# A decoder step on one Trainium2 core: first combine from the samples' tile, block vectors asked for in another order

## The reference

```python
for layer in range(DEPTH):
    np_ = rmsnorm(xp, norm_mix[layer]); ns_ = rmsnorm(xs, norm_mix[layer])
    mp, ms = mixer(np_), mixer(ns_)          # layer 0 attention, layer 1 s5_mix
    xp = xp + mp; xs = xs + ms
    xp = xp + hier_moe(rmsnorm(xp, norm_ffn[layer]), *moe_w)
    xs = xs + hier_moe(rmsnorm(xs, norm_ffn[layer]), *moe_w)
y_prompt = rmsnorm(xp, norm_final)
```

## Time and profile before

| | us |
|---|---|
| median of 3 runs | 935.3 |
| lowest, highest | 932.11, 938.24 |
| profiled execution | 935.06 |
| its span | 933.3 |

### The profile page before, as it was taken

How to read it: one execution, slowest core, us unless ns; L and a number is a source line. 1 busy time by engine, 2 the same in 40 slices (tenths; PEclk the granted TensorE clock), 3 DMA queues, 4 the chain that set the end, 5 groups by cost and what they waited for, 6 DMA issues and landing times.

```text
span 933.3 us, 12709 instructions
## 1 busy us (share of the span) xinstructions
PE 759.3 (81%) x4843; PEld 471.9 (51%) x4843; DVE 405.6 (43%) x1001; ACT 260.0 (28%) x554; POOL 151.7 (16%) x233
## 2 busy tenths in 40 slices
PE   3899977988999889997800599899999889999730
PEld 2344445857545775554500477544345487555420
DVE  3378695866678441111155567301112262111118
ACT  6020035644122102322231356310014412232203
POOL 1010003000868012332000201000000001333110
PEclk9999996999999799999965799899999979999875
DMA  9462135000632898999789377780131296999936
GB/s 343 138 210 89 51 137 192 2 1 7 217 136 114 331 408 330 408 411 403 272 280 316 44 193 185 198 325 0 45 135 46 75 402 246 405 409 406 375 138 226
DMA packets 75382, 201.81 MB, mean 216 GB/s; under 512 B 14873, under 2 KB 29593, under 8 KB 74265
## 3 DMA queue, kind: packets, MB, share of 16 engines
q1 hardware_dynamic: 58360, 161.77, 48.1%
q0 software_dynamic: 9696, 19.75, 6.0%
q10 hardware_dynamic: 7264, 19.46, 5.7%
HBM read 171.64 MB, written 39.39 MB: 226 GB/s over the span
## 4 chain that ended last, share of the span: by engine, by line
PE 61%; DMA 14%; DVE 10%; ACT 7%; SPq 4%; issue 2%; PEldq 0%; POOL 0%; DVEq 0%; PEld 0%; POOLq 0%; ACTq 0%
PE PSUM L2025 14%; PE PSUM L1832 9%; PE PSUM L1617 8%; PE PSUM L1776 7%; PE PSUM L1853 4%; DMA RING<-in_moe_w_up 3%; DMA RING<-in_attn_w_qkv 3%; PE PSUM L1820 3%; PE PSUM L1574 2%; DMA PH<-in_moe_w_up 2%; DVE X L1495 2%; DMA RING<-XNT 2%; PE PSUM L1975 2%; PE PSUM L1971 2%; SPq L467 2%
## 5 line engine op out<-in xcount | busy, mean ns | idle before, releaser
L1617 PE MATMUL PSUM<-RING,XNT 128*128 128x512 f32 (+2 forms) x256 | 94.5, 567 | 4.1 <-DMA RING<-in_attn_w_qkv 3.4
L1832 PE MATMUL PSUM<-PH 128*64 128x256 f32 x448 | 87.4, 404 | 9.0 <-DMA PH<-in_moe_w_up 5.1
L2025 PE MATMUL PSUM<-PH,XNT 128*128 128x512 f32 (+1 forms) x220 | 88.1, 593 | 0.3 <-PE PSUM L2025 0.3
L657 POOL DMA_INDIRECT PH<-xn_scratch,PH x32 | 32.6, 1020 | 340.7 <-DVEq L1440 247.5
L1832 PE MATMUL PSUM<-RING,PH 128*64 128x256 f32 x384 | 71.2, 398 | 9.7 <-DMA PH<-in_moe_w_up 5.0
L1471 DVE TENSOR_TENSOR PH<-PH,PSUM 128x128 f32<-128x128 f32 x32 | 9.3, 289 | 137.1 <-ACT PH L962 137.1
L1617 PEld LDWEIGHTS PSUM<-RING,XNT 128*128 128x128 f32 (+1 forms) x256 | 40.4, 177 | 53.7 <-issue 47.7
L1832 PEld LDWEIGHTS PSUM<-PH 128*64 128x64 f32 x448 | 52.4, 146 | 28.3 <-issue 12.5
L1776 PE MATMUL PSUM<-RING,PH 128*128 128x512 f32 (+1 forms) x160 | 62.6, 593 | 0.0
L2025 PEld LDWEIGHTS PSUM<-PH,XNT 128*128 128x128 f32 (+1 forms) x220 | 36.4, 180 | 47.9 <-issue 47.8
L1556 DVE TENSOR_TENSOR PH<-PSUM,PH 128x512 f32<-128x512 f32 (+1 forms) x10 | 6.9, 690 | 116.4 <-ACT PH L1066 116.4
(11 more groups left out here) (378 smaller groups left out, 1359.3 us busy)
## 6 DMA issues: line engine op xcount, KB each, us to landing
PH<-in_moe_w_gate SPq DMA_DIRECT2D x28, 512.0 KB
PH<-in_moe_w_up SPq DMA_DIRECT2D x28, 512.0 KB
RING<-in_moe_w_gate SPq DMA_DIRECT2D x24, 512.0 KB
RING<-in_moe_w_up SPq DMA_DIRECT2D x24, 512.0 KB
RING<-in_moe_w_down SPq DMA_DIRECT2D x24, 512.0 KB
PH<-in_moe_w_down SPq DMA_DIRECT2D x24, 512.0 KB
RING<-in_attn_w_qkv SPq DMA_DIRECT2D x4, 1536.0 KB
XNT<-in_moe_w_gate SPq DMA_DIRECT2D x12, 512.0 KB
```

The source lines that it names most:

```text
L657: pool.indirect_dma_start(out=XG[:, i % 2, :], out_offset=None, in_=xn_d[layer], in_offset=bass.IndirectOffsetOnAxis(ap=IDX[:, i:i + 1], a ...
L1617: last = te.matmul(PSUM[lo:hi, b0 + col // 512, col % 512:col % 512 + n], XT[:, c, t * P:t * P + r], RING[:, c // 2, (c % 2) * QKV + col:( ...
L1832: last = te.matmul(PSUM[m * 64:(m + 1) * 64, 2 + i % 2, 0:2 * FF], XGT[:, i % 2, c, m * 64:(m + 1) * 64], gu[:, :, c, :], start=(c == 0), ...
L2025: last = te.matmul(PSUM[p0:p0 + r, 2 * (i % 2) + w, :], XT[:, c, t * P:t * P + r], slot(SLOT[q])[:, (2 * (c % 3) + w) * 512:(2 * (c % 3) + ...
```

## The change

Five edits. `TILES` gives the norm of layer 0's combine (n = 2) the tile order 4, 0, 1, 2, 3: the row loads, DVE's additions, both halves of the norm and the copies to AL go in that order, and `place` numbers the semaphores' values accordingly; all other norms keep theirs. SP loads two blocks' vectors behind the row loads and the other two behind the copies to AL. ACT asks for the fifth block's vectors in iteration 3 behind the copies of U, and no longer in iteration 2 behind the copies of the taps; the sixth to eighth stay. PE waits for the tenth `x_updated` (the last addition) and runs `keep_busy(16, 7)` ahead of the end of phase 4. PE runs `keep_busy(10, 7)` in iteration 0 between the transposes of W and the wait for the gather.

```diff
+        TILES = {2: (4, 0, 1, 2, 3)}
+        def tiles(n):
+            return TILES.get(n, range(NT))
+        def place(n, t):
+            return NT * n + list(tiles(n)).index(t)
         block = ctx.enter_context(nc.Block())
...
                 sp.wait_ge(S("all_stored"), layer + 1)
-                for t in range(NT):
+                for t in tiles(2 + 2 * layer):
                     sp.dma_start(YG[t][0:ROWS[t], :, :],
...
             sp.dma_start(in_d[:, 2 * GP * CH:], PWRQ.rearrange("p r k g -> p (r k g)")).then_inc(S("bb_out"), 16)
+            def block_in(k):
+                ring_load(Q_SSM + k, [(slot(SLOT[Q_SSM + k])[:, 0:BLK_F], blk_d[k])])
             experts(0)
...
             rows_back(0)
-            for k in range(4):
-                ring_load(Q_SSM + k, [(slot(SLOT[Q_SSM + k])[:, 0:BLK_F], blk_d[k])])
-            for t in range(NT):
-                sp.wait_ge(S("xn_done"), 2 * NT + t + 1)
+            for k in (0, 1):
+                block_in(k)
+            for t in tiles(2):
+                sp.wait_ge(S("xn_done"), place(2, t) + 1)
                 rows = AL[t:PCH:4, :, :] if t < 4 else AL[PCH:NCH, :, :]
                 sp.dma_start(rows, XN[0:ROWS[t], t, :]).then_inc(S("al_in"), 16)
+            for k in (2, 3):
+                block_in(k)
...
             else:
-                act.wait_ge(S("x_updated"), NT * (n - 1) + t + 1)
+                act.wait_ge(S("x_updated"), place(n, t) - NT + 1)
             r = ROWS[t]
...
                                  accum_out=SS[0:r, n, t:t + 1]).then_inc(S("squares"), 1)
-            act.wait_ge(S("squares"), NT * n + t + 1)
+            act.wait_ge(S("squares"), place(n, t) + 1)
             nc.scalar.activation(RSTD[0:r, n, t:t + 1], SS[0:r, n, t:t + 1], ACT.Sqrt, bias=EPSC[0:r, :],
...
         def norm_dve(dve, ch, n, t):
-            dve.wait_ge(S("roots"), NT * n + t + 1)
+            dve.wait_ge(S("roots"), place(n, t) + 1)
             r = ROWS[t]
             ch(nc.vector.reciprocal(RSTD[0:r, n, t:t + 1], RSTD[0:r, n, t:t + 1]))
-            if t == 0:
+            if t == tiles(n)[0]:
                 dve.wait_ge(S("gamma_in"), 16 * (n + 1))
...
                                          ).then_inc(S("hs_in"), 1)
-                for t in range(NT):
+                for t in tiles(2 + 2 * layer):
                     norm_act(act, 2 + 2 * layer, t)
...
             moe(0, 4)
+            def block_in(k):
+                q = Q_SSM + k
+                act.wait_ge(S("ring_free"), freed(q))
+                act.dma_start(slot(SLOT[q])[:, 0:BLK_F], blk_d[k]).then_inc(S(f"ring_full{SLOT[q]}"), 16)
...
                     nc.scalar.activation(uk[:, :, 0:NSEQ], ut[:, :, PCH:NCH], ACT.Copy).then_inc(S("u_ready"), 1)
+                    if k == 3:
+                        block_in(4)
                 if 2 <= k < NB + 2:
...
                     ins.then_inc(S("kp_ready"), 1)
-                    if 4 <= k + 2 < NB:
-                        q = Q_SSM + k + 2
-                        act.wait_ge(S("ring_free"), freed(q))
-                        act.dma_start(slot(SLOT[q])[:, 0:BLK_F], blk_d[k + 2]).then_inc(S(f"ring_full{SLOT[q]}"), 16)
+                    if 5 <= k + 2 < NB:
+                        block_in(k + 2)
                 if k >= 3:
...
                                            ).then_inc(S("ov_dve"), 1)
-                for t in range(NT):
+                norm = 2 + 2 * layer
+                for j, t in enumerate(tiles(norm)):
                     r = ROWS[t]
...
                                                 in1=X[0:r, t, :], op0=ALU.mult, op1=ALU.add).then_inc(S("yg_used"), 1)
-                        dve.wait_ge(S("yg_used"), (layer * NT + t) * 2 + k + 1)
+                        dve.wait_ge(S("yg_used"), (layer * NT + j) * 2 + k + 1)
                     dve.sem_inc(S("x_updated"), 1)
-                    if t:
-                        norm_dve(dve, ch, 2 + 2 * layer, t - 1)
-                norm_dve(dve, ch, 2 + 2 * layer, NT - 1)
+                    if j:
+                        norm_dve(dve, ch, norm, tiles(norm)[j - 1])
+                norm_dve(dve, ch, norm, tiles(norm)[-1])
                 end_phase(dve, ph)
...
                     last.then_inc(S("st_transposed"), 1)
+                    pe.wait_ge(S("x_updated"), 2 * NT)
+                    keep_busy(16, 7)
                 end_phase(pe, ph)
...
                 last.then_inc(S("w_transposed"), 1)
+                if k == 0:
+                    keep_busy(10, 7)
                 pe.wait_ge(S("u_gathered"), k + 1)
...
                     pe.wait_ge(S("u_ready"), k)
```

## The result

The changed kernel takes 929.62 us (median of 13 runs, 925.76 to 938.66), the kernel before 934.65 us (13 runs, 931.68 to 945.91). The ratio is 0.9942, with a 95% interval of 0.9916 to 0.9969: by the ratio 5.4 us less, between 2.9 and 7.9. It is faster, but by less than the 1% that the prediction set for "faster", and by half of the forecast 11.2 us. The time lies in the range of 920 to 931 us. The profiled execution took 925.76 us (span 923.8), the shortest of the 13, so its stages stand at the favourable end.

What follows compares the result with a forecast made beforehand. The prediction took a DMA queue, carrying XN's tiles into AL behind four blocks' loads, to bound the seam. Terms -7.2 - 3.0 - 0.7 - 1.0 + 0.7 = -11.2 took 935.06 to 923.9 us; range 920 to 931.

Steps and rivals of the forecast that it cites:

- the seam: Between layer 0's experts and the state-space loop: 19.44 us waiting on XN's transfer into AL, expected to become 6 to 8.
- the fifth block later: In the loop: its later-requested load lands 0.9 us after its transposes' present start, costing +0.7 us, bounds 0 and +2.
- the forecast's own part: Total time if the forecast holds, without the rivals: 920 to 926.5 us around 923.9, chance 0.62.
- rival one: At the copies to AL: full tiles serialise behind the samples' tile, taking 15.3 us; total 929.5 us, chance 0.20.
- Two blocks moved behind the tiles: In SP's queue: 3.01 MB no longer stand ahead of the tiles, -7.2 us; what the moved blocks meet costs nothing.
- the start-up: At the first row loads: 1.2 us of slow starting, which could hide the samples' slow load; 0.7 counted, 0.5 left.
- The samples' tile first: At the copies to AL: it holds half the engines while others move full tiles; 10.75 us instead of 13.75, -3.0.
- its row load first: At the combine's row loads: the samples' slow load falls into the start-up, -0.7 us, between 0 and -1.2.
- The fillers: On PE before the loop: they keep the clock up, so the first block runs at 2.4 GHz, -1.0 us.
- rival two: In the loop: the fifth block's load meets shift pieces and sixth block, landing 4 us late; 927.2 us, chance 0.08.

Runs made afterwards that it cites:

- split_only: The kernel before with only its third and fourth blocks' loads moved behind the tiles' copies; 927.84 us, ratio 0.9925.
- natural_order: The changed kernel with layer 0's combine tiles in order 0 to 4 again, the samples' tile last; 934.32 us, ratio 0.9976.
- one_ahead: The changed kernel with only one block's vectors loaded ahead of the tiles' copies and three behind; 929.98 us, ratio 0.9942.
- fifth_old_again: A repeat, with a second profile, of the changed kernel with the fifth block's load back at its old place in iteration 2; 926.64 us, ratio 0.9903.
- fifth_old_place: The changed kernel with the fifth block's load back at its old place, behind the KP copies of iteration 2; 924.16 us, ratio 0.9854.

## Why the prediction was half right

The mechanism of the seam was right, the sum there a little large, and one step behind it, *the fifth block later*, was sized wrongly by far. The time lies within 920 to 931 us only because that range was stretched over the rivals; the forecast's own part ended at 926.5. That 929.62 us is the time of rival one (929.5) is chance: the tiles did not serialise, and GpSimd's copy came 36.6 us behind the first row load, 509.3 in the times of the earlier trace rows, between the forecast's 507.5 and the rival's 511 to 512. Point by point:

- **Two blocks moved behind the tiles, -7.2.** The blocks end 7.7 us earlier (7.2 and 0.5 of the start-up). Alone, in the natural order of the tiles, it brought 5.7 us (split_only): there it is not so that what the moved blocks meet costs nothing. Queued behind the samples' tile as the last one, they lengthen its tail, 15.4 us for the tiles instead of 13.75 (natural_order).
- **The samples' tile first, -3.0, and its row load first, -0.7.** Together 2.6 to 3.4 us at the seam (natural_order against the profiles of the changed kernel), near the 3.7. But not for the reason given: the tiles take 12.6 us, not 10.75, because the samples' tile ahead of the others holds all engines at 120 GB/s for 5 us. The half share that I argued from the earlier trace rows was that of a transfer with nothing behind it. Rival one's 15.3 us is further off on the other side, and its two instructions of 16 engines each do not fit the half share of the samples' tile in the earlier trace rows. The Trainium skill, "SBUF — State Buffer", section "Can I just issue two DMAs to hit both halves?", has two transfers to different partitions serialise nearly wholly. The 12.6 us lie between that and full overlap. The 1.7 us that the blocks add to a tail in the natural order make up the difference.
- **The fillers, -1.0: nothing.** The barrier fell near 505 and the last filler ended at 508.4, both as forecast when counted from the first row load (3.2 us later in this execution). But the rows came 5.2 us behind it instead of 3.2, because the seam was 1.9 us longer than forecast. The clock stayed at 1.00 through 4.6 idle us and fell 0.6 us before the work began. Where the rows come sooner (one_ahead) half of the step holds: the first transposes of U take 0.72 us instead of 1.22.
- **The fifth block later, +0.7: about +5.** This is the step that failed. The load itself came as forecast (PE waited 0.89 us for it), though it was asked for only 2.9 us later than in fifth_old_again, counted from the first row load, and not 4.2. The step priced what the pieces do to the load, from the row where it moved beside them, and not what the load does to the pieces. The prediction's rival two named the company, pieces and sixth block, but let the load be the late one. With the load cut to a sixteenth, or moved back, the time falls to 923.7 and 924.4 us. Its price varies from one execution to the next: the longest step exceeds 9.5 us by 1.3 to 8.6 us in five profiles, and the medians give about 5.
- **Not foreseen: -2.4 in the first outputs.** The pieces of the first block land 3.19 us after their last issue, before 4.09, and the outputs then take 4.8 us at 1.00 of the clock where they took 6.3 before, half of it at 0.50. Why the pieces came later before is not shown, and there is only one profile of that kernel. Below, the kernel before (timeline and chain of waits); the changed kernel waits 0.68 us there (above).

```profile
532.50 0.66 PE L1971 MATMUL PSUM<-PH,XNT 128*72 128x128 f32 x4 [2.45 <-DMA PH<-PH]
```

```profile
533.75 0.76 PE PSUM L1971 x4
534.50 1.06 PE PSUM L1975 x8
535.57 1.06 PE PSUM L1971 x4
```

Summed: -5.7 - 3.0 + 0 - 2.4 + 5.2 = -5.9 us, against -5.4 measured. Without the fifth's new place it is -11.1, and 924.4 us were measured. The agreement to half a microsecond says little, since the first terms come from single profiles and the last from medians.

That the forecast of 923.9 us is so near the 924.4 us of the kernel without the fifth's new place is partly luck: the blocks (1.5), the samples' tile and its row load (0.7) and the fillers (1.0) were taken too large, and the first outputs, which gave 2.4, were not foreseen.

**What stays open.** That the fifth load, 1.3 us behind the first of the third block's pieces and with the sixth load close behind, makes pieces late is shown by taking it away. How they are held up inside the DMA engines is not: no run tells a piece's place in its queue from slow writes. Nor does a run move the sixth load alone. That the load asked for next takes part is suggested by the two latest groups: the last piece landed 0.2 us after that load, 559.98 and 559.8 us in natural_order, 568.91 and 568.7 us in fifth_old_place. Nor is it known why one execution loses 1.3 us and another 8.6, and why at the old place some executions are late in a later step (17.5, 12.9 and 10.2 us in three of five profiles), where the loads are 9.5 us apart.

## What to carry to other kernels

When a transfer is moved in time, price both sides of its new company: how late it lands itself, and how late it makes the small transfers that move beside it and that someone waits for. A row of a transfer with nothing behind it in the queue says nothing of its rate with something behind it. And where a loop's stall comes and goes, one profile can sit anywhere in its spread: compare the steps of the loop in several profiles before costing a stage.

## What the runs showed of the hardware that I had not expected

- A 256 KB copy into eight partitions used half the engines at 52 GB/s when it was last; with 1472 KB loads queued behind it, all engines were busy and 94 to 99 GB/s moved; ahead of 512 KB copies 120 GB/s moved, theirs included.
- The same copy on another queue, beside loads to 128 partitions, brought the sum of both from 417 GB/s down to 185 to 249.
- The third group of eight 64 KB copies landed 6.7 to 11.8 us after its last issue beside two 1472 KB loads issued 5.6 us apart (five profiles), and 2.8 to 3.9 us in eight other profiles. That loads further apart do no harm is not so: the fifth group, between loads 9.5 us apart, landed after 3.6 to 9.7 us.
- TensorE's granted clock stayed at 1.00 through 4.6 us without work and fell to 0.50 then, 0.6 us before work began again (513.0 and 513.62 us).
